# A gated-delta chunk inverse on Trainium2: chunks 3 to 8 write the masked V of a head pair as one 128x128 block with zero quadrants, and form X and Q of a pair in one product

## The reference

```
def wkv7_scan(s0, r, w, k, v, a, b):
    def step(s, inp):
        r_t, w_t, k_t, v_t, a_t, b_t = inp
        sa = jnp.einsum('bhij,bhj->bhi', s, a_t)
        s = s * w_t[:, :, None, :] + sa[..., :, None] * b_t[..., None, :] + v_t[..., :, None] * k_t[..., None, :]
        y = jnp.einsum('bhij,bhj->bhi', s, r_t)
        return s, y
```

## Time and profile before

| | |
|---|---|
| three runs | 1065.58, 1065.11, 1059.28 us; median 1065.11 |
| the profiled execution's own time | 1064.27 us |
| its span in the profile | 1062.5 us |
| granted TensorE clock, mean | 0.984 of full speed |
| TensorE (PE) busy | 985.0 us, 93% |
| weight loads (PEld) busy | 728.9 us, 69% |
| VectorE (DVE) busy | 552.9 us, 52% |
| ScalarE (ACT) busy | 374.0 us, 35% |
| GpSimd (POOL) busy | 461.4 us, 43% |

### The profile page before, as it was taken

How to read it: one execution, slowest core, us unless ns; L and a number is a source line. 1 busy time by engine, 2 the same in 40 slices (tenths; PEclk the granted TensorE clock), 3 DMA queues, 4 the chain that set the end, 5 groups by cost and what they waited for, 6 DMA issues and landing times. The chain is left out here.

```text
span 1062.5 us, 22807 instructions
## 1 busy us (share of the span) xinstructions
PE 985.0 (93%) x9433; PEld 728.9 (69%) x9433; DVE 552.9 (52%) x1176; ACT 374.0 (35%) x764; POOL 461.4 (43%) x505
## 2 busy tenths in 40 slices
PE   5999999979989989999999999999998999997885
PEld 4777787768878778888787888884554555554442
DVE  6587776757666527777455465333374222221125
ACT  3444446546666524444344440100121111111013
POOL 7647565257868457877732344410001222221110
PEclk9999999989999999999999999999998999999997
DMA  8022221030000056420351224408888999999985
GB/s 270 0 85 80 85 85 40 0 87 5 4 4 5 4 139 183 141 64 2 106 159 42 78 79 159 159 0 312 365 323 339 414 415 415 415 416 415 411 342 236
DMA packets 86000, 182.86 MB, mean 172 GB/s; under 512 B 9897, under 2 KB 59589, under 8 KB 78218
## 3 DMA queue, kind: packets, MB, share of 16 engines
q1 hardware_dynamic: 79325, 168.59, 43.7%
q0 software_dynamic: 5088, 8.43, 2.1%
q10 hardware_dynamic: 1485, 4.39, 1.1%
HBM read 172.98 MB, written 17.55 MB: 179 GB/s over the span
## 5 line engine op out<-in xcount | busy, mean ns | idle before, releaser
L2429 POOL DMA_INDIRECT d_y<-tl_xn,ex_sidx x32 | 32.1, 1002 | 113.2 <-DVE tl_xn L3021 105.6
L2424 POOL DMA_INDIRECT tl_xn<-d_tok,ex_gidx x16 | 16.9, 1053 | 139.4 <-DVEq L3012 76.5
L3017 DVE SCALAR_TENSOR_TENSOR ex_sg<-tl_psA,ex_slot_rs,ex_sg 128x128 f32<-128x128 f32 x32 | 11.2, 351 | 124.6 <-ACT ex_sg L2788 124.5
L264 PE MATMUL psv<-xT,w_sum 128*128 128x260 f32 x256 | 61.7, 384 | 1.2 <-DVE uv_gu L1702 0.6
L226 POOL TENSOR_TENSOR w_sum<-w 128x512 f32<-128x512 f32 x16 | 21.2, 1327 | 94.2 <-PE mg_w L264 94.0
L2788 ACT ACTIVATE ex_sg<-tl_psA,ex_slot_rs 128x128 f32<-128x128 f32 x32 | 11.8, 368 | 123.4 <-PE tl_psA L2622 122.1
L264 PEld LDWEIGHTS psv<-xT,w_sum 128*128 128x128 f32 x256 | 48.3, 190 | 9.9 <-issue 1.3
L264 PE MATMUL rk_ps<-xT,rk_w 128*128 128x260 f32 x208 | 50.1, 384 | 0.0
L264 PE MATMUL rk_ps<-xS,rk_w 128*128 128x260 f32 x200 | 48.6, 386 | 0.0
L264 PEld LDWEIGHTS rk_ps<-xT,rk_w 128*128 128x128 f32 x208 | 39.3, 190 | 6.7 <-issue 0.8
L264 PEld LDWEIGHTS rk_ps<-xS,rk_w 128*128 128x128 f32 x200 | 37.4, 190 | 8.0 <-issue 2.5
(11 more groups left out here) (637 smaller groups left out, 2713.6 us busy)
## 6 DMA issues: line engine op xcount, KB each, us to landing
wd<-in_moe_w_down SPq DMA_DIRECT2D x13, 1024.0 KB, 22.9
rk_w<-in_w_in SPq DMA_DIRECT2D x12, 1024.0 KB, 5.4
w_uv<-in_w_in SPq DMA_DIRECT2D x16, 512.0 KB, 5.3
w<-in_w_in SPq DMA_DIRECT2D x8, 1024.0 KB, 5.9
tl_x<-in_moe_w_down SPq DMA_DIRECT2D x8, 1024.0 KB, 19.0
xT<-in_moe_w_gate SPq DMA_DIRECT2D x5, 1024.0 KB
xT<-in_moe_w_up SPq DMA_DIRECT2D x5, 1024.0 KB
w<-in_proj_a SPq DMA_DIRECT2D x4, 1024.0 KB, 5.7
```

Of the source, the lines that this page charges most:

```text
L264: ins = eng.matmul(bank[:, 0:TH], w[:, k, :], x[:, k, :], start=(first and k == 0), stop=(last and k == NK // 2 - 1), skip_group_check=True)
L2424: eng.indirect_dma_start(out=xg[:, p % 2, :], out_offset=None, in_=m.d_tok, in_offset=bass.IndirectOffsetOnAxis(ap=gidx[:, p:p + 1], axis= ...
L2429: eng.indirect_dma_start(out=m.d_y2, out_offset=bass.IndirectOffsetOnAxis(ap=rows, axis=0), in_=yo[:, x, :], in_offset=None, bounds_check= ...
L3017: eng.scalar_tensor_tensor(out=sg[:, out, :], in0=psg[out][:, P:2 * P], scalar=scale, in1=sg[:, out, :], op0=ALU.mult, op1=ALU.mult).then_ ...
```

## The change

In chunks c = 2 to 7 and at the levels 0 to 3, VectorE writes the masked V of a pair not as 64 columns on each half of the partitions but as a block of 128x128 (`VB`), in which the quadrants that belong to neither head are zero. To do so it reads R twice by a broadcast and multiplies it by a mask of 128x128 for each pair (`wide_mask`). R itself is still formed by 16 products of 64x64, whose moving operand is now a half of that block. X and Q of a pair are then formed by one product with 128x128 weights, 4 for a group instead of 16. Chunks 0 and 1 and level 4 stay as they were.

The two V blocks lie in the tokens 0 to 127 of br and k, and the masks in the tokens 0 to 127 of kk and v, which nothing reads any more by then. GpSimd writes the masks (`wide_masks`), half of them in chunk 0 and half in chunk 1, ahead of `with_diagonal`. R's place in PSUM is spread out, so that one access pattern reads all pairs of a group (`out_r`).

```diff
--- before.py
+++ after.py
@@ -918,6 +918,8 @@
         XQ = sb("ck_XQ", [P, NP, 2, CH])
         Vs = [sb(f"ck_V{n}", [P, NP, CH]) for n in range(2)]
         V = Vs[0]
+        VB = [m.br[:, :, 0:P], m.k[:, :, 0:P]]
+        FIRST_WIDE, WIDE_LEVELS, WIDE_OPS = 2, 4, 5
         rh = sb("ck_rh", [P, NP, HD])
         st = sb("ck_st", [P, NP, HD])
         sh = m.lora_in[0:3 * NSH, 0:3 * P].rearrange("r (n c) -> r n c", n=3)
@@ -926,7 +928,7 @@
         XB = [ps(f"ck_x{g}", [P, 2, 512]) for g in range(G)]
         s_step, s_zero, s_px, s_pi, s_bk, s_fin, s_sto, s_out = \
             (sem("k_" + n) for n in ("step", "zero", "px", "pi", "bk", "fin", "sto", "out"))
-        s_lw, s_sv, s_sh, s_sv_e, s_sh_e, s_t2 = (sem("k_" + n) for n in ("lw", "sv", "sh", "sv_e", "sh_e", "t2"))
+        s_lw, s_sv, s_sh, s_sv_e, s_sh_e, s_t2, s_wide = (sem("k_" + n) for n in ("lw", "sv", "sh", "sv_e", "sh_e", "t2", "wide"))
         first_v, first_u = m.w_uv[:, 0, 0], m.w_uv[:, 0, 1]
 
         def pair_sems(name):
@@ -963,7 +965,7 @@
             return other if t and lv % 2 else own
 
         def out_r(g, t, n):
-            return RB[g][:, t, n * CH:(n + 1) * CH]
+            return RB[g][:, t, n * 4 * CH:n * 4 * CH + CH]
 
         def out_xq(g, t, n):
             return XB[g][:, t, n * 2 * CH:(n + 1) * 2 * CH]
@@ -983,6 +985,15 @@
         def running(c, first, last):
 
             return m.cum[:, :, c * (CH + 1) + first:c * (CH + 1) + last]
+
+        def wide(c, lv):
+            return c >= FIRST_WIDE and lv < WIDE_LEVELS
+
+        def wide_mask(lv):
+            return (m.kk, m.v)[lv // 2][:, lv % 2 * GP:(lv % 2 + 1) * GP, 0:P]
+
+        def wide_at(t, rows):
+            return hi if (rows == hi) != bool(t) else lo
 
         def a_rows(eng, c, g, rows, which):
             eng.wait_ge(s_px, c)
@@ -1095,16 +1106,28 @@
                     old_y(c, g)
                 eng.wait_ge(s_w_e[g], c * NL + lv + 1)
                 V = Vs[(lv + 1) % 2]
+                W = VB[(lv + 1) % 2]
                 if lv < NL - 1:
                     for t, n, p, own, other in heads(g):
                         at, to = rows_at(t, lv, own, other), rows_at(t, lv + 1, own, other)
-                        last = eng.matmul(out_r(g, t, n)[to], XQ[at, p, 1, :], V[at, p, :], start=True, stop=True)
+                        v = V[at, p, :] if not wide(c, lv) else W[at, p, wide_at(t, at)]
+                        last = eng.matmul(out_r(g, t, n)[to], XQ[at, p, 1, :], v, start=True, stop=True)
                     last.then_inc(s_w[g], 1)
                 if lv == 0:
                     eng.wait_ge(s_bkt[g], c + 1)
                     eng.wait_ge(s_v_e[g], c * 2 + 2)
                 if lv in (3, 4):
                     eng.wait_ge(s_rh_e[g], 2 * c + lv - 2)
+                if wide(c, lv):
+                    for t in range(2):
+                        for n in range(HP):
+                            p = g * GP + t * HP + n
+                            if lv < NL - 2:
+                                last = eng.matmul(out_xq(g, t, n), W[:, p, :], XQ[:, p, :, :], start=True, stop=True)
+                            else:
+                                last = eng.matmul(out_xq(g, t, n)[:, 0:CH], W[:, p, :], XQ[:, p, 0, :], start=True, stop=True)
+                    last.then_inc(s_x[g], 1)
+                    return
                 for t, n, p, own, other in heads(g):
                     at, to = rows_at(t, lv, own, other), rows_at(t, lv + 1, own, other)
                     if lv < NL - 2:
@@ -1303,11 +1326,19 @@
             def masked_r(c, lv, g):
                 V = Vs[(lv + 1) % 2]
                 eng.wait_ge(s_w[g], c * NL + lv + 1)
-                if lv == 0:
+                if wide(c, lv):
+                    if c == FIRST_WIDE and lv == 0:
+                        eng.wait_ge(s_bk, 4 * FIRST_WIDE)
+                        eng.wait_ge(s_wide, 2 * WIDE_OPS)
+                    r = b64(RB[g][:, 0]) if lv == 0 else RB[g][:, :, :].rearrange("p t (n c) -> p (t n) c", c=4 * CH)[:, :, 0:CH]
+                    eng.tensor_tensor(VB[(lv + 1) % 2][:, grp(g), :].rearrange("p n (h c) -> p n h c", h=2),
+                                      r.unsqueeze(2).to_broadcast([P, GP, 2, CH]),
+                                      wide_mask(lv).rearrange("p n (h c) -> p n h c", h=2), ALU.mult).then_inc(s_w_e[g], 1)
+                elif lv == 0:
                     eng.tensor_tensor(V[:, grp(g), :], b64(RB[g][:, 0]),
                                       m.levels[:, 1, :].unsqueeze(1).to_broadcast([P, GP, CH]), ALU.mult).then_inc(s_w_e[g], 1)
                 else:
-                    eng.tensor_tensor(by_type(V[:, grp(g), :]), two(RB[g], CH),
+                    eng.tensor_tensor(by_type(V[:, grp(g), :]), two(RB[g], 4 * CH, slice(0, CH)),
                                       m.levels[:, lv + 1, :].unsqueeze(1).unsqueeze(1).to_broadcast([P, 2, HP, CH]),
                                       ALU.mult).then_inc(s_w_e[g], 1)
 
@@ -1375,6 +1406,19 @@
                 eng.tensor_tensor(st[:, grp(g), :], st[:, grp(g), :],
                                   running(c, CH, CH + 1)[:, grp(g), :].to_broadcast([P, GP, HD]), ALU.mult).then_inc(s_st[g], 1)
 
+            def wide_masks(c):
+                t_ = (m.kk, m.v)[c]
+                for g in range(G):
+                    eng.wait_ge(s_tb[g], c + 1)
+                eng.memset(t_[:, :, 0:P], 0.0).then_inc(s_wide, 1)
+                eng.wait_ge(s_wide, c * WIDE_OPS + 1)
+                for rows in (lo, hi):
+                    for t in range(2):
+                        out = t_[rows, :, wide_at(t, rows)].rearrange("p (l t n) c -> p l t n c", l=2, t=2)[:, :, t]
+                        eng.tensor_copy(out, m.levels[rows, 2 * c + 1:2 * c + 3, :].unsqueeze(2).to_broadcast([HD, 2, HP, CH]))\
+                           .then_inc(s_wide, 1)
+                eng.wait_ge(s_wide, (c + 1) * WIDE_OPS)
+
             def summed_y(c, g):
                 y = m.r[:, grp(g), tokens(c)]
                 eng.wait_ge(s_y_e[g], c + 1)
@@ -1403,6 +1447,8 @@
                     r_rows(eng, c + 1, g, hi, 1)
                 for g in range(G):
                     eng.wait_ge(s_ar[g], 4 * c + 4)
+                if c < FIRST_WIDE:
+                    wide_masks(c)
                 for g in range(G):
                     with_diagonal(c + 1, g)
                 for g in range(G):
```

## The result

| | kernel before | changed kernel |
|---|---|---|
| median | 1063.18 us (4 runs) | 1093.74 us (4 runs) |
| lowest, highest | 1059.28, 1065.58 | 1091.81, 1094.77 |
| ratio | | 1.0302, 95% interval 1.0269 to 1.0334 |
| profiled execution, its span | 1064.27, 1062.5 | 1091.81, 1090.1 |

I forecast 1073.4 us, a loss of 9; measured is a loss of 30.6 by the medians and 27.5 between the two profiled executions. The sign was right, the size wrong by a factor of three, and the time lies far outside 1066 to 1081. By the text's own bound of 1% this is slower, to which I gave 35%.

A forecast was written before the change was run, and what follows sets the result against it. TensorE was taken as the bound in the chunks, with ScalarE in levels 3 and 4. Six chunks at +1.5 us made 9.0, GpSimd's masks 0.1; 9.1 on the profiled 1064.27 gave 1073.4 us, range 1066 to 1081.

The forecast's parts named there:

- the text's own bound of 1%: Whole kernel: about 1%, 10.65 us, can be told from no change, so slower means above 1075.8 us; chance 35%.
- TensorE's stream sets the levels, and a chunk's loss goes to the end one for one: Chunks: TensorE's own stream bounds levels 1 and 2, with ScalarE levels 3 and 4; each microsecond lost reaches the end.
- A turn of four quadrants and one full product stream the same columns in the same time: X and Q blocks: 110 ns a turn, 111 ns a full product, four 0.44 us; no streaming saved.
- issue stalls: Two stalls like one of 0.71 us might go with 1152 fewer instructions: gain 0 to 3 us, taken as 0.
- Level 3 at the pace of 128-column weights: X at level 3: four products cost as much with 64 columns as with 128, some 0.2 us more.
- Joints: Gaps where the array's shape changes, some 0.14 us: R 0.38 instead of 0.28, wide block 0.62; 20 a chunk, before 8.
- VectorE's masks +0.19 a chunk, GpSimd's 0.1 in all: Only the first wider mask at level 0 is exposed, +0.19 us; GpSimd's mask writing in chunks 0 and 1, 0.1.
- The Trainium skill's 81 ns for a load and a product: Wide blocks: by this figure 0.12 us shorter each, 5.8 us over 48 blocks, total 1067.6; measured 111 ns taken instead.
- the joints cost little: Rival, 22%: 128-column weights are pulled ahead while quadrants run; 0 to +1 us a chunk, 1064 to 1070 us.
- instructions are the bound: Rival, 5%: X and Q's 0.44 us is instruction handling; each block saves some 0.3 us, 1047 to 1054 us.
- joints drag their neighbours: Rival, 13%: ScalarE and VectorE get X and V later, TensorE waits for copies at levels 0 and 3; 1080 to 1085 us.

The follow-up runs named there:

- the experiment with transposes: The changed kernel with each wide product replaced by one transpose of a 128x128 block, the inverse not computed: 1070.72 us, ratio 1.0094 to the kernel before.

## Why the prediction was wrong, by its steps

- **TensorE's stream sets the levels, and a chunk's loss goes to the end one for one**: right. Chunks +31.2 us, rest of the span -3.9, no more than it varies by anyway. And where the narrow products ran twice, 18.6 us of added stream cost 16.
- **"A turn of four quadrants and one full product stream the same columns in the same time"**: this step failed. It holds for one instruction. But the 16 narrow instructions of a block are 8 products, four side by side, and the wide ones are 4 products of two instructions. I set four instructions of 111 ns where eight run. The missed term is 48 blocks x 4 x 0.111 = 21.3 us; 9.1 + 21.3 = 30.4 against 30.6 measured. That the two sums meet within 0.2 us is partly luck, since the interval of the ratio leaves the loss between 28.6 and 35.5 us. But the experiment with transposes puts 8 to 10 us on what I had counted and leaves 20 to 22 for what I had not, and it fits stage by stage in chunk 3: level 0 took 2.96 us (290.47 to 293.43) for my 2.00, levels 1 and 2 8.38 for 6.48, level 3 2.85 for 1.96, the last group 0.91 for 0.94. These are 3.7 us more than the sum, and 8 blocks x 4 x 0.111 are 3.6. The two totals that tell it stand in the earlier trace rows, x64 for L1533, and in the kernel, 32 calls. The 1152 fewer instructions that the prediction set beside the issue stalls are 768 by the same count.
- **Level 3 at the pace of 128-column weights**: right in kind (1.04 us a block, and 0.61 with 64-column pieces), again with four instructions for eight.
- **Joints**: right. R 0.39 for 0.38; the eight-instruction block 1.09 for 0.62 + 0.44 = 1.06. With the first mask and level 3 the sum was 9.0 us for six chunks; the kernel that has all these with four-instruction blocks measured 8 to 10. The 19.2 us a chunk that the forecast periods were set against held an issue stall of 0.71 us; without one a chunk is 18.7 to 18.9.
- **VectorE's masks +0.19 a chunk, GpSimd's 0.1 in all**: together nothing measurable (1.0006) where the products are narrow. The later masks hid beside TensorE's blocks; the first one does delay R, by 0.25 us, and in that kernel it takes the place of a wait for ScalarE (129.9 us for the seven periods in both).
- **The Trainium skill's 81 ns for a load and a product** is not what this stream did: 111 ns an instruction here too, in fp32. The Trainium skill gives this figure without a type.
- **The rivals**: that the joints cost little (22%) and that instructions are the bound (5%) are refuted: the first by the transposes (1.3 to 1.4 us more a chunk), the second by the blocks themselves, where eight instructions take 1.09 us and sixteen narrow ones 0.44. That joints drag their neighbours (13%) had the right direction and the wrong cause: ScalarE's copies waited for TensorE (43.0 us in all behind L1126), and TensorE's waits for ScalarE fell from 5.9 to 3.7 us (240 to 410 us of the span). The true case, that the wide product itself streams twice as long, was not among my cases, because the miscounted row had excluded it.

## What to carry to other kernels

Before a duration from a row becomes a price for one call, divide the row's count by the calls that the code makes: for fp32 products the trace has two instructions each, for `eng.transpose` one. Then count how much of the array the useful work fills. Joining two 64x64 products into one 128x128 block with zero quadrants halves the instructions and doubles the time of the stream, if four such products stood side by side before. Changing the array's shape between neighbours cost 0.1 to 0.15 us each time here and should be counted, but it was the smaller part, and taking such changes away did not make the kernel faster.

## What the runs showed of the hardware

- A full-array fp32 instruction with only 64 columns to stream takes about as long as with 128: L1128 eight in 1.10 us, L1126 eight in 1.16. With weights of 64 columns, two side by side, the block of sixteen instructions is 0.61 us with 64 columns to stream and 0.92 to 1.02 with 128.
- A transpose of 128x128 fp32 data is one instruction: the block of four takes 0.58 us up to the next product, with a mean weight load of 141 ns at line 1030 of the kernel before, against 191 ns for the real weights of L1126.
- Doubling VectorE's output from 256 to 512 elements a partition on 48 masks (690 instead of 418 ns, 13 us in all) changed the time by 0.4 us (-1.4 to 2.7): an engine off the bound has that much room here.
